# Two blocks on one core: slimmer attention heads on DVE, one modulation vector of the second block formed in the first feed-forward stage

## The chip, the cores and the metric

The kernel runs on one core of a Trainium2 chip. The metric is the device time of one execution in microseconds (us), lower is better. The median of three runs before the change is 3611.9 us (3607.03 to 3613.27).

## What is computed

Two transformer-like blocks in float32 on 256 latent tokens and 256 context tokens of width 2048. Both are steered by modulation vectors: `silu(c) @ w_ada + b_ada` has 6 x 2048 columns in the first block, `silu(c_2) @ w_mod_2 + b_mod_2` as many in the second.

```python
# first block
hl = rmsnorm(x) * (1 + sc_m) + sh_m;  x = x + g_m * mixer(hl @ w_in)      # SSD, pooling, Fourier branches
x = x + g_f * swiglu(rmsnorm(x) * (1 + sc_f) + sh_f)                      # feed-forward, width 5632
x = rmsnorm(x, final_norm_w)
# second block
sh_m, sc_m, gt_m, sh_f, sc_f, gt_f = split(silu(c_2) @ w_mod_2 + b_mod_2, 6)
p_lat, p_ctx = h_lat @ w_in_2, h_ctx @ w_in_2
x = x + gt_m * (concat([hgrn2(p), window_attention(p)]) @ w_out_2)
x = x + gt_f * swiglu(modulate(rms_norm(x), sh_f, sc_f))
# window attention, per head: keys are 256 context and 256 latent tokens, 8 query heads, 2 key heads
probs = softmax(concat([scores_with_mask, sink]));  o = probs[:-1] @ v
```

## The kernel before

Every product is made in three float32r matmuls: a weight piece (128 x 1024, 512 KB) is loaded by SP into one of four `raw` buffers, ACT casts it to `whi` (`stage`, L1348), DVE forms `wlo = raw - whi` (`stage`, L1771), and TensorE multiplies each 128 x 128 part of it as `wlo*xhi + whi*xhi + whi*xlo` (`product`). There are three pairs of split buffers, and pieces are staged two ahead of their use (`AHEAD`). A piece holds 8 parts, 24 matmuls.

The order of all work is written by one plan, `schedule()`. It goes through the tiles of the large products in sequence, and each engine's function then runs through the same list of beats, doing its share of each. So the order on every engine is fixed, and an engine waits in order. For each 128 x 128 part `flowed()` adds `3 * n / 2300` to two counters, n being the columns streamed (256 here, so 0.334 "planned us", the unit of all paces). When the second counter reaches `s.pace[1]`, `tick()` takes one beat from the background list `s.back`; the first does the same with `s.pace[0]` and the foreground jobs (attention heads, HGRN heads, context rows).

The background list holds the modulation vectors, `mods(s, layer, js)`. A vector is 2 halves x 16 `mod` steps, then a `modsum` per half. A step is one 512 KB DMA from POOL's queue (L842) into one of two buffers and, on DVE, a multiply-add of 128 x 1024 into an accumulator (L1702, the first of a half L1783): one for vectors 2 to 5, two for vectors 0 and 1, which are formed for the latent and the context condition both. A `modsum` is 8 small products with a column of ones on TensorE per accumulator, and an addition on DVE (L1793). `s.need(layer, j)` forces the rest of the list where a vector must be ready.

Before the change the first feed-forward stage (`ffn(0, ...)`, planned us 887 to 1592) forms vector 5 of block one and vectors 0 and 1 of block two at a pace of 5.9. `ctx2`, the normalisation of the context rows of block two, needs vector 1 and starts at planned us 1477.6 in that stage; the last step of vector 1 is at 1480.2. Vectors 2, 3 and 4 follow at 4.2 from the HGRN stage on (`end 5`, planned us 1635); vector 4 has its steps from 1923 to 2058, the last 19 of them in the attention stage, which starts at 1977. The final projection's second half is from 2062 to 2105 (`out2b`), and the second feed-forward stage follows.

In the attention stage eight heads (`attend`, ten beats each, up to four heads at a time, taken in turns) run beside the query projections `aq` and the first half of the output projection `out2a`. The scores of a head are two tiles of 128 queries x 512 keys (`way_sc[w]`). On DVE: `head` (a reciprocal, L2240, and a product), `rope` (L2247, L2249, L2252), then for each of the two tiles scale and mask (L1702, from PSUM), row maximum (L2278) and the larger of it and the sink, negated (L2280); in the next beat, for each tile, the sum of the denominators (L2285), its reciprocal (L2287) and the scaling of the probabilities (L2289). On ACT: the square (L1654), the root (L1657), for each tile the exponential with its row sum (L1677) and the sink's exponential (L1678), later the copies of the transposed probabilities out of PSUM (L1684). TensorE transposes the probabilities and forms the output `ao` in PSUM. DVE copies it to SBUF (L2294), ACT casts that copy (L1688) and DVE subtracts (L2297), which gives the split input of the projection.

## Time and profile before

| | |
|---|---|
| profiled execution | 3611.78 us, its span 3610.0 us |
| busy, share of the span | PE 3466.7 us (96%), DVE 2414.1 (67%), ACT 1555.8 (43%), POOL 172.7 (5%) |
| chain that ended last | PE 86%, DVE 9%, ACT 3%, issue 2%, DMA 1% |
| mean granted TensorE clock | 0.977 |
| mean traffic | 203 GB/s |
| DVE L1771, the splits | 990 operations, 1191.1 us |
| DVE L1702, weight sums of 128 x 1024 | 488 operations, 542.6 us |

PE busy is the time in which a matmul was under way; matmuls are pipelined and their ends are modelled. The chain is followed back from the last instruction of the program, at each step to what released it. "Idle before" is time in which an engine stood still ahead of a group, and the releaser is what ended it. A granted clock of 1.00 is 2.4 GHz, of 0.5 is 1.2 GHz; a value between is a mean over a stretch with both.

### The profile page before, as it was taken

How to read it: one execution, taken by the hardware profiler on the slowest of the kernel's cores; microseconds unless marked ns; L12 is line 12 of the kernel's file. 1: busy time of each engine (PE TensorE's matmuls, PEld its weight loads, DVE VectorE, ACT ScalarE, POOL GpSimd, SP SyncE). 2: the span in 40 equal slices, each digit the busy share in tenths (PEclk: the TensorE clock that was granted, in tenths of full speed). 3: DMA queues.
4: the chain of work that ended last, by engine and by line, in shares of the span. 5: the costliest groups of instructions: out<-in, count | busy, mean ns of one | idle time of the engine just before them, and what ended most of it. 6: DMA issues, size and time to landing. Idle time of an engine off the chain costs nothing.

```text
span 3610.0 us, 58459 instructions
## 1 busy us (share of the span) xinstructions
PE 3466.7 (96%) x24888; PEld 3200.9 (89%) x24888; DVE 2414.1 (67%) x2995; ACT 1555.8 (43%) x2184; POOL 172.7 (5%) x328
## 2 busy tenths in 40 slices
PE   7889999999999989999999989999988999999999
PEld 3477788699999989999998968888987899999999
DVE  6777666466777676778777466777697666445544
ACT  2244554443433344433334444555454444334443
POOL 0000000000000000000000001000000000000000
PEclk9999999999999999999999999999999999999999
DMA  7632224478887767778776647555553577565565
GB/s 284 235 117 72 83 96 134 154 242 272 275 280 262 255 228 258 259 250 268 245 244 210 183 145 251 175 181 177 176 181 118 176 260 263 179 188 186 186 185 177
DMA packets 201428, 731.90 MB, mean 203 GB/s; under 512 B 22352, under 2 KB 22608, under 8 KB 200656
## 3 DMA queue, kind: packets, MB, share of 16 engines
q1 hardware_dynamic: 153792, 551.20, 45.5%
q0 software_dynamic: 46656, 171.99, 15.3%
q8 instruction: 196, 3.21, 0.3%
q10 hardware_dynamic: 720, 4.98, 0.3%
q14 instruction: 64, 0.52, 0.0%
HBM read 725.98 MB, written 2.10 MB: 202 GB/s over the span
## 4 chain that ended last, share of the span: by engine, by line
PE 86%; DVE 9%; ACT 3%; issue 2%; DMA 1%; ACTq 0%; DVEq 0%
PE ps L859 85%; DVE t L1702 4%; DVE wlo L1771 2%; ACT whi L1348 1%; DVE hT L1702 1%; PE ps L1024 1%; DVE t L2240 0%; DMA res<-in_xT 0%; DVE res L1702 0%; DVE t L2278 0%; DVE t L1880 0%; DVE hT L2044 0%; DMA t<-in_w_ada 0%; DVE hT L2010 0%; DVE t L2001 0%
## 5 line engine op out<-in xcount | busy, mean ns | idle before, releaser
L859 PE MATMUL ps<-hT,whi 128*128 128x256 f32 (+1 forms) x11360 | 2205.6, 294 | 0.0
L859 PEld LDWEIGHTS ps<-hT,whi 128*128 128x128 f32 x11360 | 1797.4, 189 | 59.7 <-issue 6.5
L859 PE MATMUL ps<-hT,wlo 128*128 128x256 f32 (+1 forms) x5680 | 1711.5, 301 | 53.3 <-DVE wlo L1771 19.2
L1771 DVE TENSOR_TENSOR wlo<-raw,whi 128x1024 fp32r<-128x1024 f32 (+1 forms) x990 | 1191.1, 1206 | 820.4 <-ACT whi L1348 818.8
L1348 ACT ACTIVATE whi<-raw 128x1024 fp32r<-128x1024 f32 (+1 forms) x990 | 1029.2, 1042 | 929.8 <-PE ps L859 925.2
L859 PEld LDWEIGHTS ps<-hT,wlo 128*128 128x128 f32 x5680 | 1076.4, 190 | 110.8 <-issue 72.8
L859 PE MATMUL ps<-t,whi 128*128 128x256 f32 x3136 | 562.7, 282 | 0.0
L1702 DVE SCALAR_TENSOR_TENSOR t<-t,misc 128x1024 f32<-128x1024 f32 (+1 forms) x488 | 542.6, 1139 | 18.9 <-DMA t<-in_w_mod 13.7
L859 PEld LDWEIGHTS ps<-t,whi 128*128 128x128 f32 x3136 | 484.6, 190 | 0.4
L859 PE MATMUL ps<-t,wlo 128*128 128x256 f32 x1568 | 446.2, 285 | 5.9 <-DVE wlo L1771 5.9
L859 PEld LDWEIGHTS ps<-t,wlo 128*128 128x128 f32 x1568 | 297.7, 190 | 7.1 <-DVE wlo L1771 4.9
L859 PE MATMUL ps<-t 128*128 128x32 f32 (+4 forms) x1088 | 219.4, 351 | 17.2 <-ACT t L1684 9.1
L859 PEld LDWEIGHTS ps<-t 128*128 128x128 f32 x1088 | 165.9, 201 | 52.1 <-issue 20.5
L859 PE MATMUL ps<-whi,hT 128*128 128x512 f32 (+1 forms) x640 | 188.0, 380 | 0.0
L842 POOL DMA_DIRECT2D t<-in_w_mod x192 | 102.7, 535 | 1472.7 <-DVE t L1702 1001.3
L859 PE MATMUL ps<-wlo,hT 128*128 128x512 f32 (+1 forms) x320 | 127.7, 399 | 19.2 <-DVE wlo L1771 18.2
L859 PEld LDWEIGHTS ps<-whi,hT 128*128 128x128 f32 x640 | 119.2, 193 | 25.0 <-issue 1.4
L1503 ACT ACTIVATE t<-t 128x256 fp32r<-128x256 f32 x88 | 36.7, 418 | 232.3 <-DVE t L2092 232.3
L859 PE MATMUL ps<-t,cst 128*128 128x256 f32 (+1 forms) x318 | 95.9, 416 | 21.2 <-DVE t L1702 6.4
L842 POOL DMA_DIRECT2D t<-in_w_ada x128 | 67.5, 528 | 753.7 <-DVE t L1702 577.5
L1496 ACT ACTIVATE t<-ps 128x256 f32<-128x256 f32 x88 | 33.9, 385 | 147.6 <-PE ps L859 147.6
L859 PEld LDWEIGHTS ps<-wlo,hT 128*128 128x128 f32 x320 | 62.0, 194 | 33.7 <-DVE wlo L1771 19.6
(213 smaller groups left out, 1579.3 us busy)
## 6 DMA issues: line engine op xcount, KB each, us to landing
raw<-in_w_in_s SPq DMA_DIRECT2D x250, 512.0 KB, 4.7
t<-in_w_mod POOLq DMA_DIRECT2D x192, 512.0 KB, 4.8
raw<-in_w_ffn_gu SPq DMA_DIRECT2D x176, 512.0 KB, 5.1
raw<-in_w_gu SPq DMA_DIRECT2D x176, 512.0 KB, 4.5
t<-in_w_ada POOLq DMA_DIRECT2D x128, 512.0 KB, 5.3
t<-in_w_ada_s SPq DMA_DIRECT2D x64, 512.0 KB, 4.7
raw<-in_w_out SPq DMA_DIRECT2D x64, 512.0 KB, 4.5
raw<-in_w_ffn_down SPq DMA_DIRECT2D x64, 512.0 KB, 4.2
```

Of the source, the lines that this page charges most:

```text
L842: e.dma_start(b, w[k * P:(k + 1) * P, a:a + PIECE]).then_inc(*up(S.sem("mod", layer, j, half, k), layer, j, half, k, n=16))
L859: return e.matmul(o, l, r, start=start, stop=stop)
L1024: ins = e.transpose(ps(i), src(i), idn)
L1348: fn(S.buf("split", p)[0][:, 0:n], S.buf("raw", p)[:, 0:n], ACT.Copy).then_inc(*up("hi", p))
L1496: fn(S.buf("gf", layer, m), S.buf("ps", t)[:, 0:T], ACT.Silu).then_inc(*up("ffn_a", "g", layer, m))
L1503: fn(F[layer]["hid"][0][:, i, :], S.buf("gf", layer, m), ACT.Copy).then_inc(*up("ffn_a", "hid", layer, m))
L1702: return e.scalar_tensor_tensor(out=o, in0=a, scalar=s, in1=b, op0=op0, op1=op1)
L1771: tt(lo[:, 0:n], S.buf("raw", p)[:, 0:n], hi[:, 0:n].bitcast(F32), ALU.subtract).then_inc(*up("lo", p))
```

## The change

One. In the heads DVE takes one maximum over both tiles, one comparison with the sink, one sum and one reciprocal for both tiles; the scratch columns of `way_st` are laid out anew. ACT makes one exponential of the sink for both tiles, and takes over the scaling of the probabilities (a Copy with a scale per partition). The transposes wait for ACT's scaling. The copy of `ao` to SBUF is left out: ACT casts from PSUM and DVE subtracts from PSUM.

Two. Vector 2 of block two joins the first feed-forward stage, whose pace goes from 5.9 to 4.7. There the steps of vector 0 now run from planned us 1048.8 to 1199.1, of vector 1 from 1208.4 to 1359.0, of vector 2 from 1368.4 to 1518.6. The list of the second block starts with vector 3; it is empty at planned us 1918, before the attention stage starts. The memory for vector 2 is that of the ring and the accumulator of that stage. Nothing else of the plan moves.

```diff
@@ -332,11 +332,12 @@
                 s.lin("res", (f"down{layer}{half}", m), [(down, m, half)], T)
 
     def before0():
-        s.pace[:] = [3.0, 5.9]
+        s.pace[:] = [3.0, 4.7]
 
         def run():
             yield from mods(s, 0, [5])
             yield from mods(s, 1, [0, 1])
+            yield from mods(s, 1, [2])
 
         s.back = run()
 
@@ -365,7 +366,7 @@
     values(0)
     s.finish()
     s.add("end", 5)
-    s.back = mods(s, 1, [2, 3, 4])
+    s.back = mods(s, 1, [3, 4])
     s.pace[:] = [3.2, 4.2]
     s.aux = "aux_c"
     s.add("hg_in")
@@ -701,13 +702,14 @@
     F = [ffn_memory(f3), None]
     mod_memory((0, 5), f3, 2, 2)
     mod_rings[1, 0], accs[1, 0] = mod_rings[0, 5], accs[0, 5]
+    mod_rings[1, 2], accs[1, 2] = mod_rings[0, 5], accs[0, 5]
     c2tmp, c2sq = ring(2, lambda: carve(T), f3), ring(2, lambda: carve(T), f3)
     c2rs = carve(T)
     rs2, rs3 = (mod_rings[0, 5][0].t[:, i * T:(i + 1) * T] for i in range(2))
     leave()
 
     scope()
-    mod_memory((1, 2), f5, 2, 1)
+    mod_memory((1, 3), f5, 2, 1)
     cat = carve3(8, T)
     evf = [ring(2, lambda: carve(512), f5) for _ in range(2)]
     scope()
@@ -756,8 +758,8 @@
             b.after = ("norm_v", f"ffn{i}", 12 + n)
     n2_tmp = [Buf(b.t, None, f4) for b in F[0]["tp"]]
     sq_rings = {"out": gt[0:3], "down01": F[0]["sq"], "n2": F[0]["sq"], "out2b": [Buf(b.t, None, ("fence", 8)) for b in rawq]}
-    acc_bufs = {st: [Buf(a, None, f) for a in accs[st]] for st, f in (((0, 2), f2), ((0, 5), f3), ((1, 2), f5), ((1, 5), f7))}
-    acc_bufs[1, 0] = acc_bufs[0, 5]
+    acc_bufs = {st: [Buf(a, None, f) for a in accs[st]] for st, f in (((0, 2), f2), ((0, 5), f3), ((1, 3), f5), ((1, 5), f7))}
+    acc_bufs[1, 0] = acc_bufs[1, 2] = acc_bufs[0, 5]
 
     CTX, LAT, ALL = slice(0, T), slice(T, 512), slice(0, 512)
     streams = ((cin, rstd0[:, 0:T], CTX), (xR, rstd0[:, T:2 * T], LAT))
@@ -772,7 +774,7 @@
         return ap.unsqueeze(2).to_broadcast([P, ap.shape[1], n])
 
     def mod_stage(layer, j):
-        return (layer, j) if (layer, j) in mod_rings else (layer, 2 if j > 1 else 0)
+        return (layer, j) if (layer, j) in mod_rings else (layer, 2 + layer if j > 1 else 0)
 
     def done(t):
 
@@ -1279,7 +1281,7 @@
             for i in range(2):
                 S.take(rings["aux_c"], "pT", h, i)
                 ps = S.buf("pT", h, i)
-                g.wait_ge(*S.freed("pT", h, i), *at("at_v", "p", h, i))
+                g.wait_ge(*S.freed("pT", h, i), *at("at_a", "pn", h, i))
                 turn(lambda c: ps[:, c * P:(c + 1) * P], lambda c: way_sc[w][:, i, c * P:(c + 1) * P], 4).then_inc(*up("at_pe", "pT", h, i))
             yield
             S.take(rings["aux_c"], "ao", h)
@@ -1669,14 +1671,15 @@
             yield
             yield
             yield
-            snk = sm("attn_sink_2", h, 1)
+            o, sc = way_st[w], way_sc[w]
+            g.wait_ge(*at("at_v", "max", h))
             for i in range(2):
-                b, o = 8 * i, way_st[w]
-                sc = way_sc[w][:, i, :]
-                g.wait_ge(*at("at_v", "max", h, i))
-                fn(sc, sc, ACT.Exp, bias=o[:, b + 1:b + 2], accum_out=o[:, b + 2:b + 3]).then_inc(*up("at_a", "p", h, i))
-                fn(o[:, b + 3:b + 4], snk, ACT.Exp, bias=o[:, b + 1:b + 2]).then_inc(*up("at_a", "sink", h, i))
-            yield
+                fn(sc[:, i, :], sc[:, i, :], ACT.Exp, bias=o[:, 2 + i:3 + i], accum_out=o[:, 4 + i:5 + i]).then_inc(*up("at_a", "p", h, i))
+            fn(o[:, 6:8], o[:, 2:4], ACT.Exp, bias=sm("attn_sink_2", h, 1)).then_inc(*up("at_a", "sink", h))
+            yield
+            for i in range(2):
+                g.wait_ge(*at("at_v", "inv", h))
+                fn(sc[:, i, :], sc[:, i, :], ACT.Copy, scale=o[:, 10 + i:11 + i]).then_inc(*up("at_a", "pn", h, i))
             yield
             yield
             for i in range(2):
@@ -1684,8 +1687,8 @@
                 fn(way_pT[w][:, :, i * P:(i + 1) * P], S.buf("pT", h, i).rearrange("p (c n) -> p c n", c=4), ACT.Copy).then_inc(*up("at_a", "pT", h, i))
                 S.free("pT", h, i, by=("at_a", "pT", h, i))
             yield
-            g.wait_ge(*at("at_v", "o", h), *done_of("vtok", 0))
-            fn(hT[0][:, 8 + h, CTX], way_sc[w][:, 0, 0:T], ACT.Copy).then_inc(*up("at_a", "cat", 8 + h))
+            g.wait_ge(*at("at_pe", "ao", h), *done_of("vtok", 0))
+            fn(hT[0][:, 8 + h, CTX], S.buf("ao", h)[:, 0:T], ACT.Copy).then_inc(*up("at_a", "cat", 8 + h))
 
         run(beats, {"rms_in": rms_in, "ada_sum": ada_sum, "ada_h": ada_h, "stage": stage, "silu": silu, "btok": btok, "xtok": xtok, "ev_dt": ev_dt, "dt": dt, "ssd": ssd, "ev_z": ev_z,
                     "ev_tok": ev_tok, "pool_fourier": pool_fourier, "ev_gate": ev_gate, "ev_res": ev_res, "ffn_in": ffn_in,
@@ -2270,31 +2273,24 @@
             yield
             snk = sm("attn_sink_2", h, 1)
             for i in range(2):
-                b = 8 * i
                 g.wait_ge(*at("at_pe", "s", h, i), *at("am_in"))
                 stt(sc[:, i, :], S.buf("s", h, i), P ** -0.5, amask[:, i, :], ALU.mult, ALU.add).then_inc(*up("at_v", "s", h, i))
                 S.free("s", h, i, by=("at_v", "s", h, i))
-                g.wait_ge(*at("at_v", "s", h, i))
-                e.tensor_reduce(o[:, b:b + 1], sc[:, i, :], AX.X, ALU.max).then_inc(*up("at_v", "max0", h, i))
-                g.wait_ge(*at("at_v", "max0", h, i))
-                ts(o[:, b + 1:b + 2], o[:, b:b + 1], snk, -1.0, ALU.max, ALU.mult).then_inc(*up("at_v", "max", h, i))
-            yield
-            for i in range(2):
-                b = 8 * i
-                g.wait_ge(*at("at_a", "sink", h, i))
-                tt(o[:, b + 4:b + 5], o[:, b + 2:b + 3], o[:, b + 3:b + 4], ALU.add).then_inc(*up("at_v", "den", h, i))
-                g.wait_ge(*at("at_v", "den", h, i))
-                e.reciprocal(o[:, b + 4:b + 5], o[:, b + 4:b + 5]).then_inc(*up("at_v", "inv", h, i))
-                g.wait_ge(*at("at_v", "inv", h, i))
-                ts(sc[:, i, :], sc[:, i, :], o[:, b + 4:b + 5], None, ALU.mult).then_inc(*up("at_v", "p", h, i))
-            yield
-            yield
-            yield
-            g.wait_ge(*at("at_pe", "ao", h))
-            e.tensor_copy(sc[:, 0, 0:T], S.buf("ao", h)[:, 0:T]).then_inc(*up("at_v", "o", h))
-            S.free("ao", h, by=("at_v", "o", h))
+            g.wait_ge(*at("at_v", "s", h, 1))
+            e.tensor_reduce(o[:, 0:2], sc, AX.X, ALU.max).then_inc(*up("at_v", "max0", h))
+            g.wait_ge(*at("at_v", "max0", h))
+            ts(o[:, 2:4], o[:, 0:2], snk, -1.0, ALU.max, ALU.mult).then_inc(*up("at_v", "max", h))
+            yield
+            g.wait_ge(*at("at_a", "sink", h))
+            tt(o[:, 8:10], o[:, 4:6], o[:, 6:8], ALU.add).then_inc(*up("at_v", "den", h))
+            g.wait_ge(*at("at_v", "den", h))
+            e.reciprocal(o[:, 10:12], o[:, 8:10]).then_inc(*up("at_v", "inv", h))
+            yield
+            yield
+            yield
             g.wait_ge(*at("at_a", "cat", 8 + h))
-            tt(hT[1][:, 8 + h, CTX], sc[:, 0, 0:T], hT[0][:, 8 + h, CTX].bitcast(F32), ALU.subtract).then_inc(*up("at_v", "cat", 8 + h))
+            tt(hT[1][:, 8 + h, CTX], S.buf("ao", h)[:, 0:T], hT[0][:, 8 + h, CTX].bitcast(F32), ALU.subtract).then_inc(*up("at_v", "cat", 8 + h))
+            S.free("ao", h, by=("at_v", "cat", 8 + h))
 
         run(beats, {"ada": ada, "norm_in": norm_in, "ada_tr": ada_tr, "ada_h": ada_h, "begin": begin,
                     "stage": stage, "mod": mod, "modsum": modsum, "ev_dt": ev_dt, "dt": dt, "ev_conv": ev_conv, "ssd": ssd,
```

In the middle of the attention stage, DVE's order around one head's softmax before (`t<-ps,t 128x512` is scale and mask, `t<-t,misc 128x1024` a step of a weight sum):

```order
L1771 TENSOR_TENSOR wlo<-raw,whi 128x1024
L1702 SCALAR_TENSOR_TENSOR t<-ps,t 128x512
L2278 TENSOR_REDUCE t<-t 128x1
L2280 TENSOR_SCALAR t<-t,small 128x1
L1702 SCALAR_TENSOR_TENSOR t<-ps,t 128x512
L2278 TENSOR_REDUCE t<-t 128x1
L2280 TENSOR_SCALAR t<-t,small 128x1
L1702 SCALAR_TENSOR_TENSOR t<-t,misc 128x1024
L1702 SCALAR_TENSOR_TENSOR res<-ps,modv,res 128x256
L1771 TENSOR_TENSOR wlo<-raw,whi 128x1024 x2
L2247 TENSOR_TENSOR t<-t 128x256
L2249 TENSOR_TENSOR t<-ps,t 128x256
```

and the same place in the changed kernel:

```order
L1774 TENSOR_TENSOR wlo<-raw,whi 128x1024
L1705 SCALAR_TENSOR_TENSOR t<-ps,t 128x512 x2
L2280 TENSOR_REDUCE t<-t 128x2
L2282 TENSOR_SCALAR t<-t,small 128x2
L1705 SCALAR_TENSOR_TENSOR res<-ps,modv,res 128x256
L1774 TENSOR_TENSOR wlo<-raw,whi 128x1024 x2
L2250 TENSOR_TENSOR t<-t 128x256
L2252 TENSOR_TENSOR t<-ps,t 128x256
L2255 TENSOR_TENSOR t<-t 128x256
```

One maximum and one comparison take the place of two each, and the step between the comparison and the residual addition is gone.

ACT's order around the softmax of a head late in that stage, before (L1677 exponential, L1678 sink, L1684 copy of the transposed probabilities, L1348 cast of a weight piece):

```order
L1677 ACT_TABLE_LOAD
L1677 ACTIVATE t<-t 128x512
L1678 ACTIVATE t<-small,t 128x1
L1677 ACTIVATE t<-t 128x512
L1678 ACTIVATE t<-small,t 128x1
L1654 ACTIVATE t<-t 128x256
L1348 ACTIVATE whi<-raw 128x1024
L1684 ACTIVATE t<-ps 128x4x128 x2
L1348 ACTIVATE whi<-raw 128x1024
```

and now (L1682 is the scaling that DVE did before, L1687 the copies, L1350 the cast):

```order
L1677 ACT_TABLE_LOAD
L1677 ACTIVATE t<-t 128x512 x2
L1678 ACTIVATE t<-t,small 128x2
L1656 ACTIVATE t<-t 128x256
L1350 ACTIVATE whi<-raw 128x1024
L1687 ACTIVATE t<-ps 128x4x128 x2
L1350 ACTIVATE whi<-raw 128x1024
L1682 ACTIVATE t<-t 128x512 x2
```

Both exponentials now stand ahead of the one for the sink, and the scaling stands among the casts.

DVE's order in the first feed-forward stage, gate and up tiles, while vector 1 of the second block is formed, before (L2092 and L2095 are the product with the gate and the low half of it, `t<-t,misc 128x1024 x2` is one step):

```order
L2092 TENSOR_TENSOR t<-ps,t 128x256
L2095 TENSOR_TENSOR t<-t 128x256
L1771 TENSOR_TENSOR wlo<-raw,whi 128x1024 x2
L1702 SCALAR_TENSOR_TENSOR t<-t,misc 128x1024 x2
L1771 TENSOR_TENSOR wlo<-raw,whi 128x1024 x2
L1702 SCALAR_TENSOR_TENSOR t<-t,misc 128x1024 x2
L2092 TENSOR_TENSOR t<-ps,t 128x256
L2095 TENSOR_TENSOR t<-t 128x256
L1771 TENSOR_TENSOR wlo<-raw,whi 128x1024 x3
L1702 SCALAR_TENSOR_TENSOR t<-t,misc 128x1024 x2
L1771 TENSOR_TENSOR wlo<-raw,whi 128x1024
L2092 TENSOR_TENSOR t<-ps,t 128x256
```

and now (L2095, L2098):

```order
L2095 TENSOR_TENSOR t<-ps,t 128x256
L2098 TENSOR_TENSOR t<-t 128x256
L1774 TENSOR_TENSOR wlo<-raw,whi 128x1024 x2
L1705 SCALAR_TENSOR_TENSOR t<-t,misc 128x1024 x2
L1774 TENSOR_TENSOR wlo<-raw,whi 128x1024 x2
L1705 SCALAR_TENSOR_TENSOR t<-t,misc 128x1024 x2
L2095 TENSOR_TENSOR t<-ps,t 128x256
L2098 TENSOR_TENSOR t<-t 128x256
L1774 TENSOR_TENSOR wlo<-raw,whi 128x1024
L1705 SCALAR_TENSOR_TENSOR t<-t,misc 128x1024 x2
L1774 TENSOR_TENSOR wlo<-raw,whi 128x1024 x2
L1705 SCALAR_TENSOR_TENSOR t<-t,misc 128x1024 x2
```

These rows have two steps between one product with the gate and the next before as after; over the stretch it was one or two, and is two or three.

## Rows read from the trace of the kernel before

**Rows 1.** The chain that ended last, in order of time: start us, us, what.

```profile
1291.07 636.25 PE ps L859 x5336
```

**Rows 2.** Busy time by stretches: length, PE, PEld, DVE, ACT, POOL (instructions), clock, DMA share, GB/s.

```profile
944.00:1160.00 216.00, 216.00 (x1837) 216.00 (x1837) 154.22 (x158) 84.90 (x96) 21.11 (x40) 1.00 0.83 280
1925.00:1992.00 67.00, 58.80 (x420) 54.33 (x419) 43.28 (x64) 32.14 (x55) 0.53 (x1) 0.95 0.60 185
2612.00:2632.00 20.00, 12.83 (x84) 11.18 (x84) 17.19 (x19) 9.73 (x20) 1.06 (x2) 0.87 0.59 195
2632.00:2765.00 133.00, 122.88 (x854) 111.02 (x853) 117.34 (x188) 70.90 (x114) 8.00 (x15) 0.96 0.53 172
2765.00:2786.00 21.00, 12.02 (x39) 8.52 (x40) 11.54 (x31) 7.98 (x21) 0.00 (x0) 0.72 0.04 15
```

**Rows 3.** The chain within 2600 to 2790, in order of time.

```profile
2618.66 1.28 DVE t L1702
...
2764.79 0.61 DVE t L1702
...
2775.05 0.61 DVE t L1702
```

**Rows 4.** Groups by shape, 2610 to 2786: busy us, mean ns, idle before and releaser.

```profile
L1771 DVE TENSOR_TENSOR wlo<-raw,whi 128x1024 fp32r<-128x1024 f32 x32 | 39.0, 1220 | 11.3 <-ACT whi L1348 11.3
L1348 ACT ACTIVATE whi<-raw 128x1024 fp32r<-128x1024 f32 x32 | 33.2, 1048 | 8.9 <-PE ps L859 8.8
L1702 DVE SCALAR_TENSOR_TENSOR t<-t,misc 128x1024 f32<-128x1024 f32 x19 | 24.3, 1278 | 1.2 <-DMA t<-in_w_mod 1.2
...
L1677 ACT ACTIVATE t<-t 128x512 f32<-128x512 f32 x16 | 11.6, 724 | 27.3 <-DVE t L2280 27.3
L2278 DVE TENSOR_REDUCE t<-t 128x1 f32<-128x512 f32 x16 | 11.0, 686 | 0.6
...
L2289 DVE TENSOR_SCALAR t<-t 128x512 f32<-128x512 f32 x16 | 7.8, 486 | 0.6
...
L2280 DVE TENSOR_SCALAR t<-t,small 128x1 f32<-128x1 f32 x16 | 3.4, 214 | 0.6
...
L2294 DVE COPY t<-ps 128x256 f32<-128x256 f32 x7 | 2.9, 420 | 7.0 <-PE ps L859 6.9
...
L1654 ACT ACTIVATE t<-t 128x512 f32<-128x512 f32 x2 | 1.2, 614 | 0.0
```

**Rows 5.** Who waited for whom in 2600 to 2790: us in total, times, longest us.

```profile
ACT hT L1688 <- DVE t L2294: 35.4, 8, 6.1
ACT t L1677 <- DVE t L2280: 27.3, 16, 4.6
```

**Rows 6.** DVE's instructions in order of time: start, us, what [idle before, releaser].

```profile
1852.89 0.42 DVE L2092 TENSOR_TENSOR t<-ps,t 128x256 f32<-128x256 f32 x1
1853.79 0.43 DVE L2095 TENSOR_TENSOR t<-t 128x256 fp32r<-128x256 f32 x1 [0.48 <-ACT t L1503]
1854.74 2.36 DVE L1771 TENSOR_TENSOR wlo<-raw,whi 128x1024 fp32r<-128x1024 f32 x2 [0.52 <-ACT whi L1348]
1857.02 2.48 DVE L1702 SCALAR_TENSOR_TENSOR t<-t,misc 128x1024 f32<-128x1024 f32 x2
1859.41 2.48 DVE L1771 TENSOR_TENSOR wlo<-raw,whi 128x1024 fp32r<-128x1024 f32 x2
1861.81 2.47 DVE L1702 SCALAR_TENSOR_TENSOR t<-t,misc 128x1024 f32<-128x1024 f32 x2
1864.20 0.42 DVE L2092 TENSOR_TENSOR t<-ps,t 128x256 f32<-128x256 f32 x1
```

**Rows 7.** PE's instructions in order of time: a summation of a weight sum.

```profile
1395.03 1.84 PE L859 MATMUL ps<-cst,t 128*128 128x1 f32 x16
```

**Rows 8.** DMA issues of the page: count, KB each, us to landing.

```profile
t<-in_w_mod POOLq DMA_DIRECT2D x192, 512.0 KB, 4.8
```

**Rows 9.** Who waited for whom, whole execution.

```profile
DVE t L1702 <- DMA t<-in_w_mod: 13.7, 12, 2.6
```


## The prediction

> **What bounds the kernel now.** I read the chain of waits first. It is TensorE in long clean pieces; the longest of the middle, 5336 matmuls in 636.3 us from 1291.1 on, is the first feed-forward stage, 0.119 us a matmul [rows 1]. Then the table by stretches. In 944 to 1160 the weight-sum steps of the modulation vectors already come every 4.7 planned us, at 280 GB/s, and TensorE is busy in every microsecond [rows 2]. So the memory traffic that the change asks of the feed-forward stage has been carried cleanly before, with one DVE operation per step.
>
> The same table shows the attention stage, 2612 to 2786. TensorE is idle 7.2, 10.1 and 9.0 us in its three parts (the length less PE busy), 26.3 in all; its clock is granted at 0.87, 0.96 and 0.72, so part of the time at 1.2 and not 2.4 GHz. DVE is busy 86%, 88% and 55% [rows 2]. The waits say the same from the other side: ACT stood 35.4 us for the copy L2294 and 27.3 us for the maximum L2280 [rows 5], both deep in DVE's queue, and the weight casts that TensorE needs stood behind ACT. DVE's queue is the limit, but for the last 21 us, which are a chain of single heads.
>
> **Part 1, the heads.** Per head DVE loses: one of its row maxima, against the doubled width of the other, so 2 x 0.69 against about 1.23 (0.69 for 512 columns plus 0.54, by which the 1024 wide split, 1.22, is longer); one L2280 (0.21) and, with that row as a ceiling, the second sum and the second reciprocal (0.4 together); two scalings (2 x 0.49); the copy L2294 (0.42) [rows 4]. Sum 2.2 us, for 8 heads 17 us. ACT gets two scalings of 512 columns and gives back one sink exponential. The trace has no such scaling. The nearest rows are the square at 0.61 and the exponential with its per-partition operand at 0.72 [rows 4]; the scaling has such an operand too, so I take 0.72 and keep 0.61 as the lower end: 16 x 0.72 = 11.5 us, less some 2 us for eight small operations. ACT, busy 70.9 of 133 us in the middle part [rows 2], stays near two thirds, so this hides behind TensorE; if ACT became the last to finish, it would cost up to those 9 us. The Trainium skill ("ScalarE: Activation LUTs", section "Rules for kernel authors") says to multiply on VectorE, not ScalarE. By engine time alone the rows agree (0.49 against 0.72), and by the rule this part would lose 16 x 0.23 = 4 us; but the row that decides is the one of the full queue, and that is DVE's.
>
> **Part 2, the moved vector.** 32 weight-sum steps leave the second block. The two vectors left there move up, so what the attention stage loses is all that it had: 19 steps at 1.28 us, 24 us of DVE [rows 4], and one summation by TensorE, 1.84 us as in [rows 7]; a second summation, as long, leaves the projection behind it. The HGRN stage keeps as many steps per microsecond as before: nothing there.
>
> The attention stage then comes out as follows. Start, 20 us: the chain passes through two steps of 1.28 (one is shown) [rows 3], gone: -2.5. Middle, 133 us: DVE's 117.3 us lose some 16 steps (20) and 7 heads' share (15), which leaves 82, under 70%. I let TensorE's idle time fall from 10.1 to 3 (the softmax stays, with ACT waiting for DVE and the cast waiting behind ACT), and what the slow clock costs (0.04 x 2 x 133 = 10.6 us at 1.2 GHz, up to 5.3 lost) by 3.5: -10.5. The tail: two heads of 10.26 us each (2764.79 to 2775.05) [rows 3]. Both scores must now be reduced before either exponential: two maxima and two small operations become one each (-0.4), the first exponential is no longer hidden (+0.7 to +0.8), the copy and its hand-over go (-0.45). Nothing. With the two summations the gain is 2.5 + 10.5 + 1.8 + 1.8 = 16.6 us. Ends: 6 (start and summations alone) and 22 (the middle without any idle time or slow clock).
>
> The cost lies in the first feed-forward stage. The pace there goes from a step per 5.9 to one per 4.7 planned us. In the trace a gate and up pair, 10.7 planned us, lasts 11.31 us (1852.89 to 1864.20) [rows 6], so a step comes every 4.97 us in place of 6.24. For vectors 0 and 1 a step is two DVE operations, 2.39 us of queue. Rows 6 show a period with two such steps: DVE is idle twice, 0.48 for ACT's copy and 0.52 for the cast that stands behind that copy on ACT, and busy all the rest. Neither gap can be filled, since the order is fixed. On average a period had 1.81 steps and will have 2.28; against the two of these rows it needs 0.28 x 2.39 = 0.65 us more than it has. Some 18 periods lie in such stretches (193 planned us of gate and up between the first step of vector 0 and the last of vector 1), so at most 11.7 us are missing. But DVE may fall behind: with three split buffers the cast of a piece can start two pieces (2 x 24 x 0.119 = 5.7 us) ahead, and cast and split need 1.05 + 1.22 [rows 1, 4], which leaves 3.4 us; and four double summations give DVE a pause. I take 4 us, ends 0 and 11.7. The down projections have no such gaps, and by the same rows 3.3 of splits, 0.4 of residual and 1.56 steps x 2.39 fill 7.4 of some 7.8 us: 0. Two more summations run in this stage: 2 x 1.84 = 3.7 us, in full, for TensorE is the bound [rows 1, 7].
>
> The context rows of the second block are normalised at 1925 to 1992, where TensorE is idle 8.2 of 67 us and DVE busy 43.3 [rows 2]. So far the last step came just before; now about three single steps (3.8 us) fall among DVE's operations. I take +2, ends -1 (a double summation has moved out of this stretch) and +4.
>
> **Sum.** -16.6 + 4 + 3.7 + 2 = -6.9 us against the profiled execution's 3611.8, so **3605 us**; the median of the runs shown is 3611.9, and no correction is needed. A measurement of this kernel tells 0.2%, 7.2 us, from no change.
>
> **Rivals.** (B) The overload is paid in full: 11.7 instead of 4 and 4 instead of 2 make 3615. For it: the two gaps per period are fixed. Against: 3.4 us of cover, and the pauses.
>
> (C) Slower: the steps' own DMAs come late. POOL issues the next one when its buffer, one of two, is free. A step every 4.97 us leaves 2 x 4.97 - 2.39 = 7.5 us from there to its use, where it had 10.1. A landing takes 4.8 us at the median [rows 8], but DVE stood for one up to 2.6 us, and 13.7 us in all [rows 9]. DVE waits in order, so a late landing holds the splits. It decides from landings of 7.5 us on; if the 64 double steps wait 0.4 us each, that is 26 us in a queue with nothing to spare, some 20 of them lost: 3625. Against: the clean 216 us at this pace [rows 2].
>
> (D) ACT takes DVE's place in attention: it now stands for DVE's reciprocal, with casts behind it, and the gain of the stage and its projection is 6.5: 3611.8 - 6.5 + 9.7 = 3615. For it: ACT waits in order, and it is ACT's casts that feed TensorE. Against: its 35.4 us of waiting for the copy go [rows 5]. The skill's rule above points this way.
>
> (E) Better: the middle loses all its idle and slow time (-15), a part of the tail keeps its clock (-2), the overload is covered (0) and the context rows cost nothing: -2.5 - 15 - 3.6 - 2 + 3.7 = -19.4, 3592.
>
> **How the numbers follow.** The forecast case has 0.44 (its own range 3600 to 3610, just over half of it beyond the 0.2% bound at 3604.6), B 0.17, C 0.12, D 0.10, E 0.17. Faster by over 0.2%: 0.24 + 0.17 = 0.41. Within: 0.20, 0.13 of B and 0.10 make 0.43. Slower: C and the worse end of B, 0.16. The range, 3593 to 3618, leaves out most of C and the far half of E.
>
> **What would show it.** Right: DVE under 75% busy in the middle of attention, L1688's wait for DVE gone, the stage 13 to 16 us shorter with its last two heads still some 10 us each; short waits of TensorE for wlo in the feed-forward stage, only while double steps run, and that stage 6 to 12 us longer. Wrong: a clean feed-forward stage (the cover was enough), DVE waiting for DMA there (C), ACT's waits before the casts keeping attention's length (D), or a tail that changes.

## The result

The changed kernel takes 3622.5 us at the median of 18 runs (3614.2 to 3627.8), the kernel before 3614.8 on the same chip; the ratio is 1.0027, with a 95% interval of 1.0019 to 1.0035. (The medians alone lie 7.7 us apart; the ratio is 9.8 us. One execution of the kernel before took 7763.6 us, twice the others, and the ratio leaves it out.) Forecast were 3605 and, for the range, 3593 to 3618. Its profiled execution took 3619.6 us, 7.8 more than the one of before. The page after, of its parts 1 and 4:

```profile
PE 3469.0 (96%) x24888; PEld 3201.3 (88%) x24888; DVE 2396.6 (66%) x2939; ACT 1560.9 (43%) x2192; POOL 172.8 (5%) x328
...
PE 82%; DVE 11%; ACT 4%; issue 3%; DMA 1%; ACTq 0%; DVEq 0%
```

DVE works 17.5 us less than before, as forecast, and yet has more of the chain: 11% for 9%, ACT 4% for 3%, and TensorE 82% for 86%. Work was taken from DVE, and waiting for it was added.

Where the time went I read by stages, cut at the start of the same DVE split (numbers 276, 515, ..., counted from 0) in each kernel; "idle" is TensorE without a matmul, "slow" the time at 1.2 GHz, worked out from the mean granted clock. A slow microsecond costs half of one. Since single executions differ in slow time, three profiles of each kernel are averaged, the two shown and the four repeats below:

| stage, splits | before: us (idle, slow) | after | longer by | forecast |
|---|---|---|---|---|
| up to the feed-forward stage, to 276 | 1211.4 (72.4, 48.9) | 1212.1 (71.8, 54.6) | +0.7 | 0 |
| first feed-forward, 276 to 515 | 704.3 (8.7, 22.8) | 718.7 (14.9, 26.2) | +14.4 | +7.7 |
| context rows, 515 to 560 | 148.2 (8.3, 6.8) | 150.8 (12.1, 7.9) | +2.6 | +2 |
| 560 to 600 | 138.2 | 138.2 | 0 | 0 |
| HGRN, 600 to 670 | 396.7 (0.7, 39.8) | 402.9 (0.7, 52.3) | +6.2 | 0 |
| attention, 670 to 716 | 228.9 (27.1, 23.9) | 217.7 (24.6, 12.5) | -11.2 | -16.6 |
| the rest | 780.1 | 780.1 | 0 | 0 |

The sum is +12.7; the timed runs say +9.8 (1.0027 of 3614.8; 6.9 to 12.6). The attention stage, shifted by some 6 us, against [rows 2]:

```profile
2618.00:2638.00 20.00, 18.15 (x148) 17.35 (x146) 6.45 (x11) 8.30 (x18) 0.00 (x0) 1.00 0.36 119
2638.00:2771.00 133.00, 122.29 (x878) 110.59 (x876) 93.45 (x130) 79.14 (x127) 0.00 (x0) 1.00 0.37 123
2771.00:2792.00 21.00, 9.02 (x31) 6.21 (x31) 11.23 (x22) 9.73 (x22) 0.00 (x0) 0.79 0.08 25
```

In the middle DVE fell from 117.3 to 93.5 us (I had 82), the clock is granted in full, and TensorE is idle 10.7 us, where it was idle 10.1. These two windows do not hold quite the same work, since the stage is shorter now and its start lies farther back. From the first head's row maximum to the last but one's, in the three profiles of each kernel, the heads' work is the same: 121.7 us before, with 11.1 idle, and 114.7 after, with 7.7 idle and DVE at 67%. I had let the idle time follow DVE's load, by 7.1 us down to 3; it fell by 3.4. (Both summations that leave this stage lie ahead of split 716, so the -16.6 is the whole forecast gain.) The chain that ended last within 2605 to 2835, by line, says what it follows instead; first before, then after:

```profile
by line: PE ps L859 39.9%; DVE t L1702 11.5%; DVE wlo L1771 9.7%; DVE t L2240 7.2%; issue 6.6%; ACT whi L1348 4.3%; DVE t L2278 4.2%; DVE t L2289 1.9%; ACT t L1684 1.7%; DVE res L1702 1.4%; DVE t L2280 1.3%; ACT t L1677 1.2%; DVE t L2294 1.
```

```profile
by line: PE ps L861 38.4%; DVE wlo L1774 11.7%; DVE t L2243 8.9%; ACT whi L1350 5.4%; issue 5.2%; DVE t L1705 5.0%; ACT t L1677 3.6%; DVE t L2280 3.2%; ACT t L1682 2.4%; ACT L1659 2.3%; ACT t L1687 1.7%; DVE t L2255 1.3%; DVE t L2250 1.1%; 
```

The weight-sum steps are gone from the chain (L1702 11.5%; L1705 5.0%, which is the same line's other work), but TensorE's share is no larger. The place is taken by ACT's exponential (L1677, 3.6% where it was 1.2), its new scaling (L1682, 2.4%), a table load before its root (L1659, 2.3%), and more of DVE's reciprocal of that root (L2243, 8.9% for 7.2) and of the splits (11.7% for 9.7). Who waited for whom in 2620 to 2840 after, DVE's waits and then ACT's, against [rows 5]:

```profile
DVE t L2243 <- ACT t L1659: 13.6, 5, 3.5
```

```profile
ACT t L1677 <- DVE t L2282: 30.0, 8, 4.8
...
ACT t L1682 <- DVE t L2287: 11.2, 6, 2.7
```

ACT's wait for the copy (35.4 us) is gone, as forecast. In its place stand 30.0 us for the maximum, with less work on DVE than when it was 27.3, 11.2 for the reciprocal, and a wait of DVE that before's trace does not have at all: 13.6 us for the root of the next head. One such place, DVE and ACT in order of time:

```profile
2730.15 0.17 DVE L2287 RECIPROCAL t<-t 128x2 f32<-128x2 f32 x1
2733.78 1.75 DVE L2243 RECIPROCAL t<-t 128x256 f32<-128x256 f32 x1 [3.46 <-ACT t L1659]
```

```profile
2730.35 1.34 ACT L1682 ACTIVATE t<-t 128x512 f32<-128x512 f32 x2 [2.69 <-DVE t L2287]
2731.59 0.36 ACT L1649 ACTIVATE t<-ps 128x256 f32<-128x256 f32 x1
2731.97 1.28 ACT L1659 ACT_TABLE_LOAD   x1
2733.27 0.47 ACT L1659 ACTIVATE t<-ps,misc 128x256 f32<-128x256 f32 x1
2733.64 0.38 ACT L1691 ACTIVATE hT<-ps 128x256 fp32r<-128x256 f32 x1
2733.91 2.01 ACT L1350 ACTIVATE whi<-raw 128x1024 fp32r<-128x1024 f32 x2
```

ACT stands 2.69 us for DVE's small reciprocal; then it scales, loads its table and forms the root, and for those 3.46 us DVE stands, in whose queue the next splits wait. Behind both waits stand the casts (L1350). The two engines work in turn where they had worked side by side.

### The profile page after: what moved, and what is told of

The parts are those of the page before. It is cut to its first block, busy times and chain, and to the rows that moved or that the text cites. A ratio compares the mean times of both kernels' runs of the same rounds, so it can differ in the third digit from the quotient of the medians.

```text
span 3617.7 us, 58406 instructions
## 1 busy us (share of the span) xinstructions
PE 3469.0 (96%) x24888; PEld 3201.3 (88%) x24888; DVE 2396.6 (66%) x2939; ACT 1560.9 (43%) x2192; POOL 172.8 (5%) x328
## 4 chain that ended last, share of the span: by engine, by line
PE 82%; DVE 11%; ACT 4%; issue 3%; DMA 1%; ACTq 0%; DVEq 0%
PE ps L861 81%; DVE t L1705 5%; DVE wlo L1774 3%; ACT whi L1350 2%; PE ps L1026 1%; DMA t<-in_w_ada 1%; DVE t L2243 1%; DVE hT L1705 1%; DMA res<-in_xT 0%; DVE res L1705 0%; ACT t L1677 0%; DMA t<-in_w_mod 0%; DVE t L1883 0%; DVE t L2280 0%; DVE hT L2047 0%
## 5 line engine op out<-in xcount | busy, mean ns | idle before, releaser
L1350 ACT ACTIVATE whi<-raw 128x1024 fp32r<-128x1024 f32 (+1 forms) x990 | 1028.0, 1042 | 939.1 <-PE ps L861 933.0
L1705 DVE SCALAR_TENSOR_TENSOR t<-t,misc 128x1024 f32<-128x1024 f32 (+1 forms) x488 | 542.4, 1138 | 22.9 <-DMA t<-in_w_mod 13.5
L861 PE MATMUL ps<-t,wlo 128*128 128x256 f32 x1568 | 446.7, 285 | 10.3 <-DVE wlo L1774 10.3
L861 PE MATMUL ps<-t 128*128 128x32 f32 (+4 forms) x1088 | 219.5, 351 | 17.5 <-ACT t L1687 9.7
```

The costliest lines, as they stand in the source:

```text
L861: return e.matmul(o, l, r, start=start, stop=stop)
L1350: fn(S.buf("split", p)[0][:, 0:n], S.buf("raw", p)[:, 0:n], ACT.Copy).then_inc(*up("hi", p))
L1705: return e.scalar_tensor_tensor(out=o, in0=a, scalar=s, in1=b, op0=op0, op1=op1)
```

## Experiments

**The two parts apart.** `heads_only` is the change without the moved vector (pace, lists and memory as before); `move_only` is before with the moved vector alone.

> The slimmer heads alone: the plan, the paces and the memory of the vectors are those of before. My theory after comparing the two traces: the loss lies in the moved vector, and the heads are worth about half of the 11.6 us that the attention stage lost, so 4 to 8 us less than before (ratio 0.998 to 0.999), with the first feed-forward stage and HGRN as before. The rival that ACT takes DVE's place in attention says 0 to +4 us, with ACT's waits for DVE's reciprocal (a new line in its waits) as large as the wait for L2294 that went.

> The moved vector alone, heads as before. My theory: first feed-forward stage and context rows +12 us (two more summations 4, stalls behind DVE's double steps 5 to 6, context rows 2 to 4), attention -6 to -8, so 4 to 10 us more than before (ratio 1.001 to 1.003). The rival, that HGRN's +5 us in the changed kernel belong to the heads or to chance, says +4 or less and HGRN as long as before.

Both came out at 1.0015 (1.0005 to 1.0025): 3614.4 and 3614.6 us against 3609.6. Neither part pays. The heads alone missed my expectation (4 to 8 us less). The move alone came out as expected in sum, but not in its terms: the feed-forward stage and the context rows grew by 20.7 us and not 12, and the attention stage shrank by 18.4 and not 6 to 8. With the heads alone the attention stage of the profile is 233.0 us long, 4 more than before, with 30.9 us idle; with the move alone it is 210.5, 7 shorter than with both. So the heads, meant to relieve the stage, lengthen it. DVE's waits there, heads alone:

```profile
DVE wlo L1772 <- ACT whi L1348: 33.0, 23, 2.6
DVE hT L2290 <- ACT hT L1689: 12.9, 3, 4.9
DVE t L2241 <- ACT t L1657: 12.9, 5, 3.5
```

**Another order of the steps.** `both_phase` shifts the steps in the HGRN stage by 2 planned us, `both_split` gives the single steps the faster pace and the double ones that of before:

```diff
+    s.flow[1] -= 2.0
```

```diff
+            s.pace[1] = 4.2
             yield from mods(s, 0, [5])
+            s.pace[1] = 5.9
             yield from mods(s, 1, [0, 1])
+            s.pace[1] = 4.2
             yield from mods(s, 1, [2])
```

> Both parts, and the counter behind the pace set back by 2.0 planned us at the start of the second block, so that vectors 3 and 4 have their steps where vectors 2 and 3 had them before. If the place of the steps among the HGRN beats made that stage 5 us longer, this kernel is 5 us below the changed one (ratio to before 1.001 to 1.002) and its HGRN stretch is as long as before. If the slow clock there falls by chance, it stands at the changed kernel's time within 2 us (ratio 1.002 to 1.004), and the stretch differs from execution to execution.

> Both parts, but the pace in the first feed-forward stage is 4.2 for the vectors with one sum per step (5 of block one, 2 of block two) and 5.9, as before, for vectors 0 and 1 with two. My theory that DVE's double steps at 4.7 are what stalls TensorE there: the stalls (some 5.6 us) go, the summations' 4 us stay, and context rows cost up to 4 us more since single steps now run through them densely: 3 to 6 us below the changed kernel. The rival that the stage lost its time to the summations and the clock alone: at the changed kernel's time within 2 us.

`both_phase`: 1.0034 (1.0021 to 1.0047), no gain: nothing shows that the place of the steps in the HGRN stage costs time. `both_split`: 1.0021 (1.0013 to 1.0030), the feed-forward stage 710.7 us where the change has 718.7. Of those 8.0 us, 1.8 are a half's summation that now falls behind the stage, and the context rows and the stretch behind them are 4.6 us longer, so that the timed gain, some 2 us, is below the 3 to 6 expected, and the two intervals overlap. TensorE's waits in 1215 to 1930, in the changed kernel, then with the split pace (before has one, 1.0 us):

```profile
PE ps L861 <- DVE wlo L1774: 5.1, 9, 1.3
```

```profile
PE ps L864 <- DVE wlo L1777: 2.6, 4, 1.0
```

**Which piece of the heads costs.** Three kernels on before's plan: `scale_dve` is the heads alone with the scalings back on DVE, `two_max` the heads alone with maximum and comparison tile by tile, `no_copy` is before with nothing but the copy left out. The core of the first:

```diff
-                g.wait_ge(*at("at_v", "inv", h))
-                fn(sc[:, i, :], sc[:, i, :], ACT.Copy, scale=o[:, 10 + i:11 + i]).then_inc(*up("at_a", "pn", h, i))
...
+            g.wait_ge(*at("at_v", "inv", h))
+            for i in range(2):
+                ts(sc[:, i, :], sc[:, i, :], o[:, 10 + i:11 + i], None, ALU.mult).then_inc(*up("at_v", "p", h, i))
```

> Heads of the change without the moved vector, and the two scalings of a head back on DVE; merged maximum, merged sum and reciprocal and the missing copy stay. The heads alone gave 1.0015 (1.0005 to 1.0025) of the time before and an attention stage 4.2 us longer than before in the trace, not 10 shorter. Theory S (the scaling is the cost: ACT must now stand for DVE's reciprocal, 17.3 us in the heads alone, with weight casts queued behind): the attention stage comes out 4 us or more shorter than with the heads alone, 3608 to 3611 us. Theory M (the merged maximum is the cost: neither exponential can start before both scores are reduced; ACT's wait for it was 36.6 us against 27.3 before): the stage stays about 4 us longer than before, 3612 to 3616 us, for the wait for the maximum is still there.

> Heads of the change without the moved vector, and the maximum and its comparison with the sink taken tile by tile again, so that the first exponential can start while DVE reduces the second tile; scalings stay on ACT, sum and reciprocal stay merged, the copy stays out. Theory M (merged maximum): ACT's wait for the maximum falls from 36.6 us towards 27, the attention stage is 3 to 5 us shorter than with the heads alone, 3609 to 3612 us. Theory S (scaling on ACT): no shorter than with the heads alone, 3614 us, since DVE does 0.4 us more for each head and ACT still waits for the reciprocal.

> The kernel before with one piece of the heads alone: the output of a head is cast by ACT and subtracted by DVE straight from PSUM, the copy L2294 is left out. It takes 8 x 0.42 us off DVE and one hand-over off each head, and adds nothing. Both theories S and M: attention stage 2 to 5 us shorter than before, ACT's wait before that cast far under the 35.4 us of before, 3605 to 3608 us. If the stage does not get shorter, DVE's load is not what sets it and both theories lack their ground (theory N: the trace of before was a lucky one for the clock, and heads do nothing either way).

| kernel | ratio (95%) | attention: us | idle | DVE for the root | ACT for the reciprocal | ACT for the maximum |
|---|---|---|---|---|---|---|
| before | 1 | 228.9 | 27.1 | 0 | - | 27.3 |
| heads_only | 1.0015 (1.0005 to 1.0025) | 233.0 | 30.9 | 12.9 | 17.3 | 36.6 |
| two_max | 1.0008 (0.9999 to 1.0018) | 231.3 | 28.2 | 12.9 | 17.3 | 33.1 |
| scale_dve | 0.9991 (0.9981 to 1.0002) | 223.0 | 23.7 | 0 | - | 43.0 |
| no_copy | 0.9991 (0.9981 to 1.0001) | 222.8 | 25.0 | 0 | - | 39.5 |

Theory S holds, with 3607.2 us a little under its 3608 to 3611. The groups of DVE in 2600 to 2835, heads alone and then with the scalings back:

```profile
L2241 DVE RECIPROCAL t<-t 128x256 f32<-128x256 f32 (+1 forms) x10 | 20.7, 2069 | 12.9 <-ACT t L1657 12.9
```

```profile
L2238 DVE RECIPROCAL t<-t 128x256 f32<-128x256 f32 (+1 forms) x10 | 20.7, 2065 | 0.0
```

The wait for the root comes with the scalings on ACT and goes with them, and the kernel gets 8.7 us faster (0.9991 against 1.0015) although DVE works 7.1 us more. What this shows is that the scalings do not belong at this place of ACT's order; ACT with the scalings at a later beat was not tried. Theory M has little for it: `two_max` gained 2.5 us by the ratios, within what they can tell, and the fastest two kernels have the longest waits of ACT for the maximum. That wait is where ACT happens to stand; it says nothing of the stage's length. `no_copy` came out as expected: less work on both sides of a hand-over, 5.5 us less at the medians. Its stage is 6.1 us shorter, 2.1 of them idle time and some 5 from 10.2 us less at the slow clock. Neither it nor `scale_dve` is shown to be faster than before, since their intervals reach 1.0001 and 1.0002.

**No vector moved, but a faster list.** `pace335` is before with one number:

```diff
-    s.pace[:] = [3.2, 4.2]
+    s.pace[:] = [3.2, 3.35]
```

> The kernel before, with one number changed: the steps of vectors 2, 3 and 4 of the second block come every 3.35 planned us in place of 4.2 from the HGRN stage on, so that the last is done before the attention stage starts, with no vector moved to the feed-forward stage. Theory 1 (what the move gains is the attention stage without steps, what it costs is the full DVE of the feed-forward stage): attention stage 15 to 20 us shorter as with the moved vector alone (18.3), HGRN stage 0 to 5 us longer since DVE is busy 67 to 80% there and gets 19 steps of 1.1 us more, in all 3592 to 3600 us. Theory 2 (the gain of the attention stage is a matter of where slow clock falls, and comes back elsewhere): 3605 to 3612 us.

0.9979 (0.9969 to 0.9990), 3604.2 against 3611.0 us: the attention stage is 17.5 us shorter than before (211.3; idle 18.9) and HGRN 8.9 longer (idle 4.0, slow 54.6). Theory 1 holds for the attention stage (15 to 20 us shorter). Its time (3592 to 3600 us) was missed, and the kernel lies 0.9 us from theory 2's range, because HGRN grew by more than the 5 us allowed and the stretch before it (560 to 600) by 3.7. Some 7 us of HGRN's growth are slow clock, which differs as much between profiles of one kernel (below). The same relief of the attention stage costs less in HGRN, where a step is one DVE operation, than in the feed-forward stage with its double ones.

**The whole change with the scalings on DVE, and the best parts together.** `after_scale` is the change with that one piece undone, `split_scale` adds the split pace, `p335_scale` and `p335_nocopy` add the slim heads with DVE's scalings, or the missing copy alone, to `pace335`.

> The whole change with one piece undone: the two scalings of a head are back on DVE. Theory S (scalings on ACT make DVE and ACT wait for each other in turn: in the heads alone ACT stood 17.3 us for DVE's reciprocal and DVE 12.9 us for ACT's root, which waits behind the scalings; with the scalings back on DVE and nothing else the attention stage was 9.9 us shorter, the median 7 us lower): attention stage 5 to 9 us shorter than in the changed kernel, DVE's wait for the root gone, 3612 to 3617 us, ratio 1.0005 to 1.0015. Rival (without the steps DVE has room in attention, so that the place of the scalings no longer matters): 3620 us as the whole change.

> As after_scale, and the feed-forward stage's pace split by the DVE operations of a step: 4.2 planned us for the single steps of vectors 5 and 2, 5.9 for the double ones of vectors 0 and 1. Theory O (what the moved vector costs beyond two summations is the overload of DVE while double steps come every 4.7): the stage is 3 to 5 us shorter than in after_scale, 3609 to 3613 us. Rival (the moved vector costs its time by more slow clock and traffic, whatever the order): no shorter.

> The pace of 3.35 in the second block (no vector moved; alone 0.9979 of the time before) and the slimmer heads with the scalings on DVE (alone 0.9991). Theory S: without steps in the attention stage the merged heads still take 1 to 5 us off it: 3600 to 3604 us, 0.9972 to 0.998. Rival: the gains are the same idle time counted twice, and it comes out as pace335, 0.9979, or a little slower because the merged maximum is in the chain of a head that DVE's queue no longer hides.

> The pace of 3.35 and the missing copy alone, with the heads otherwise as before. It takes work off DVE and a hand-over off each head's chain and puts nothing on ACT: attention stage 3 to 5 us shorter than with the pace alone, 3598 to 3603 us, 0.9965 to 0.9975. If the merged maximum costs nothing, p335_scale is as fast or faster; if it costs its 0.7 us per head in the chain, this one is.

| kernel | median, before beside it | ratio (95%) | attention: us (idle) | feed-forward |
|---|---|---|---|---|
| after_scale | 3612.5, 3610.4 | 1.0000 (0.9989 to 1.0011) | 207.2 (17.4) | 719.2 |
| split_scale | 3606.3 | 0.9988 (0.9979 to 0.9997) | 207.2 (15.8) | 710.6 |
| p335_scale | 3601.6 | 0.9973 (0.9963 to 0.9983) | 207.5 (15.8) | 707.0 |
| p335_nocopy | 3599.0 | 0.9968 (0.9955 to 0.9980) | 206.6 (13.2) | 703.4 |

Undoing the one piece takes the change from 1.0027 to 1.0000, with intervals that do not touch; I had expected 1.0005 to 1.0015. From the first head's maximum to the last but one's `after_scale` takes 104.6 us, 0.5 of them idle, where the change has 114.7 with 7.7 (and `move_only` 108.5 with 3.3). The chain of `after_scale` within 2605 to 2835, in order of time:

```profile
2668.52 25.66 PE ps L861 x194
2694.18 0.87 PE ps L1026 x8
2695.06 22.28 PE ps L861 x158
2717.34 0.87 PE ps L1026 x8
2718.21 14.92 PE ps L861 x106
2733.13 0.87 PE ps L1026 x8
2734.00 10.37 PE ps L861 x78
```

and the same stretch in the changed kernel:

```profile
2713.30 1.28 ACT L1659
2715.11 1.76 DVE t L2243
2717.38 1.14 DVE wlo L1774
...
2730.35 1.34 ACT t L1682 x2
2733.78 1.76 DVE t L2243
2736.38 1.14 DVE wlo L1774
```

That is what I had forecast for the change: hardly any idle time in the middle, TensorE in long pieces, 76 us nearly without a break. The split pace took another 6 us off at the medians, more than the 3609 to 3613 us expected (8.6 in the feed-forward stage of the profiles, 4.8 of it given back behind it); the two intervals overlap a little. Four kernels are faster than before by their intervals: `split_scale`, `pace335`, `p335_scale` and `p335_nocopy`. The last two came out as expected, but both intervals hold the 0.9979 of `pace335`, so what the heads add to the faster list is shown by the attention stage of the profiles (3.8 and 4.7 us shorter) and not by the times. Between those two the intervals don't tell, so the merged maximum is worth nothing that was measured.

**Repeats of both kernels,** for the baselines of the stages.

> The kernel before, a second profile. Theory C (HGRN's and the start's extra 8 us in the changed kernel's profile were chance of the clock): HGRN stage 397 to 403 us, first 276 splits 1210 to 1213 us, feed-forward stage up to the context rows 703 or 707 us, attention stage 225 to 230 us with 26 to 27 us of idle TensorE. Rival (the change makes HGRN or the start longer): HGRN 397 again.

> The kernel before, a third profile; as before_again: by theory C at least one of the two has an HGRN stage of 400 us or more, by the rival neither.

> The changed kernel, a second profile. Both: feed-forward stage up to the context rows 716 to 722 us, attention stage 216 to 219 us with 23 to 26 us of idle TensorE (11.4 shorter than before, where I had forecast some 15). Theory C: HGRN stage anywhere in 395 to 405 us; rival: 402 again.

> The changed kernel, a third profile; as after_again. By theory C the mean of HGRN over the three profiles of the change lies within 4 us of the mean of the three of before; by the rival it is 5 us longer.

HGRN took 396.9, 395.2 and 398.1 us in before, 402.1, 402.3 and 404.3 after: both of theory C's conditions, a profile of before at 400 or more and a mean within 4 us, are missed. Yet `no_copy`, `two_max`, `scale_dve` and `heads_only`, with before's order there, took 402.3, 404.8, 395.2 and 402.3, and kernels with the order of the change 398.7 to 402.2. The means of the seven profiles with each order are 399.3 and 401.1 (without `both_phase`, whose order is its own). In all of them TensorE is idle at most 1.0 us in this stage and the length follows the slow time (37.5 us slow at 395.2, 58.0 at 404.8: 9.6 us longer, where half the difference in slow time is 10.2). What places the slow periods, and so whether these 6 us belong to the change, stays open. The other stages (+14.4, +2.6, -11.2, +0.7) make 6.5 of the 9.8 us timed.

## Why the prediction was wrong

The forecast was -6.9 us, the stages say +12.7. Of the 19.6 us between them 6.7 lie in the first feed-forward stage, 5.4 in the attention stage, 6.2 in HGRN (slow clock, open) and 1.3 elsewhere.

**The attention stage: the step that failed is "I let TensorE's idle time fall from 10.1 to 3".** Its ground was that DVE's queue is the limit. The queue did get lighter (DVE under 75% busy was forecast, 70% measured), and the scaling on ACT was sized well (0.72 taken, 0.714 measured in the heads alone). But neither busy time is what the stage waits for: with the move alone, DVE at 82% left 3.3 us idle in the middle, and with both, DVE at 67% left 7.7. A wait of ACT for DVE was added in front of the casts and the root, and DVE waits for that root. I had the first half as rival D and gave it 0.10; the second, DVE waiting for ACT's root, was in no case. Undone, the idle time of the stage falls to 17.4 us (about 17 was forecast: 26.3 less 2.5 and 7.1) and the stage by 21.6 us against the profile shown, where my sum had 16.6. So the gain of the move was there, and the scalings took back 10 us of it. The start's term (-2.5) fared no better: up to the first head's maximum the stage is 1.8 us shorter, but idle 8.1 us where it was 7.7. The Trainium skill's rule to multiply on VectorE and not ScalarE ("ScalarE: Activation LUTs", "Rules for kernel authors") pointed the right way: by the durations it meant 4 us, by the runs it was 9 to 10, since the waits weigh more than the work.

**The slow clock** fell by 11.4 us in the stage, worth 5.7, where I had 3.5. **The tail:** the chain in order of time has the maxima of the last two heads at

```profile
2775.86 1.23 DVE t L2280
...
2786.15 1.23 DVE t L2280
```

10.29 us apart, where [rows 3] have 10.26: nothing, as forecast.

**The feed-forward stage: the term of 4 us for the overload was too small.** Where two matmuls start more than 0.25 us apart, the time beyond a matmul's own adds up to 14.1 us before and 22.1 after, 8 for 4 (up to 3 of the 8 may be the DMAs', see below). Behind 1295 us there are one or two such gaps in each profile of before, 0.7 us in all at most, and 11 to 16 in those of after, 7.4 to 12.0 us. A period of double steps after:

```profile
1516.25 2.48 DVE L1705 SCALAR_TENSOR_TENSOR t<-t,misc 128x1024 f32<-128x1024 f32 x2
1518.64 1.22 DVE L1774 TENSOR_TENSOR wlo<-raw,whi 128x1024 fp32r<-128x1024 f32 x1
1519.78 2.47 DVE L1705 SCALAR_TENSOR_TENSOR t<-t,misc 128x1024 f32<-128x1024 f32 x2
1522.17 0.41 DVE L2095 TENSOR_TENSOR t<-ps,t 128x256 f32<-128x256 f32 x1
```

```profile
1522.62 0.42 ACT L1505 ACTIVATE t<-t 128x256 fp32r<-128x256 f32 x1 [5.81 <-DVE t L2095]
1522.94 1.99 ACT L1350 ACTIVATE whi<-raw 128x1024 fp32r<-128x1024 f32 x2
```

Two double steps ahead of DVE's product with the gate put it late; ACT stands 5.81 us for it with two casts behind, the split waits for the first of them, and TensorE has a gap of 1.54 us at 1524. That eats the 3.4 us of cover that I had set against the overload. I counted the overload in DVE's time and the cover in TensorE's, and did not follow ACT, which passes DVE's lateness on to the casts. Waits of ACT for this product of more than 4.05 us number one in each profile of before, 14 to 16 after, two or three with the split pace; with it the time between matmuls is 15.9 us in place of 22.1, with no gap over 0.36 us behind the single steps of vector 5. So most of the loss belongs to double steps at 4.7. One long wait alone does no harm: before's ACT stood 7.8 us once, and TensorE never missed more than 0.36 us. The summations: 48 small products more run in this stage, 4.6 us in the mean; 16 of them, 1.8 us, are a half that left the context rows, so that both stages together have 2.8 us more, where I had 3.7. The rest of the 14.4, about 2 us, is time at the slow clock.

**The context rows:** +2.6 for +2; TensorE's waits for the splits rose there from 5.9 to 10.3 us, and the summation that left gave 1.8 back. **The DMAs** (rival C): over the whole execution DVE waited 13.5 us for the steps' own, before 13.7 [rows 9], and a landing now takes 5.1 us, far from C's 7.5. But the waits have moved. In the first feed-forward stage, 1215 to 1930, before has one, of 0.7 us (in its repeats none), and after

```profile
DVE t L1705 <- DMA t<-in_w_ada: 4.1, 5, 1.5
DVE t L1705 <- DMA t<-in_w_mod: 2.6, 4, 0.8
```

(9.7 and 7.3 us in its repeats). Some of TensorE's gaps stand less than 8 us behind such a wait: 0.4 us of the 7.4, 3.2 of 11.0 and 6.0 of 12.0 in the three profiles of after, and with the split pace every gap among the single steps of vector 5. So up to 3 of the 8 us are the landings' and at least some 5 the overload's: C, far from its 20 us, had a part that my sum put at nothing.

**How the cases were combined** was wrong too. B (the overload paid in full, 3615) and D (the heads give back what they take, 3615) lie in different stages and have nothing to do with each other, but I let only one happen at a time. Both together are 3611.8 - 6.5 + 11.7 + 3.7 + 4 = 3624.7, outside my range. That it is near the 3622.5 measured is partly luck: the stages it speaks of gave +5.8 and not +12.9, and HGRN's 6.2 made up for it.

## What to carry to other kernels

Work moved off the fullest engine's queue is a gain only if no new wait in turn comes with it: write down, for each engine in order, what each instruction waits for and what stands behind it, and follow a lateness through the other engine and back. An operation that must wait for DVE, set on ACT ahead of something that DVE waits for in turn, makes each stand for the other; here it was better on DVE, even where that is the fuller engine. When steps of unequal size go into a tight stretch, give each size its own pace, or put them where the size is one operation. And cases in different stages must be added, not chosen between.

## What the runs showed of the hardware

TensorE has more than one speed at a granted clock of 1.00. In 2890 to 2910, in the second feed-forward stage, nearly the same part of the program ran so before and with the pace of 3.35:

```profile
2890.00:2910.00 20.00, 20.00 (x172) 20.00 (x171) 13.35 (x13) 9.20 (x12) 1.58 (x3) 1.00 0.78 254
```

```profile
2890.00:2910.00 20.00, 20.00 (x179) 20.00 (x178) 14.69 (x15) 8.54 (x11) 1.58 (x3) 1.00 0.81 281
```

From one start to the next that is 0.118 and 0.113 us a matmul. The faster pace lasted some 100 us, from about 30 us behind split 716 on, and was worth 4.0 us; two of 18 profiles have it there (`pace335`, `after_scale`), and in the others the rest of the program took 780.1 us each time. The same pace, 179 matmuls in 20 us for 172, stands in the first feed-forward stage from 1295 on: in `before_third` for some 95 us, and in the profiles of `after` and `after_scale` for some 60. So one profile of each kernel in the table of stages has it, worth 4 and some 2.5 us, which moves the +14.4 by less than 1 us. What brings it on stayed open.

Of before alone, executions on one chip went from 3601.5 to 3620.8 us, and a stage in which TensorE was idle at most 1.0 us took 395.2 to 404.8 us. A stage's gain of a few microseconds should be read from idle time and from several profiles.
